# First attention group of a fused two-block kernel: queries and keys computed together behind zeros, x operands ahead of weight splits, second group's attention steps two slots later

## The reference

```python
def fox_mixer(h, w_in, b_f, q_gain, k_gain, w_out):        # h = rms_norm(x, mix_norm)
    q, k, v, f_logit = jnp.split(h @ w_in, [hd, 2 * hd, 3 * hd], axis=-1)
    q = rms_norm(q.reshape(bsz, seq, N_HEADS, HEAD_DIM), q_gain)     # 16 heads of 128
    k = rms_norm(k.reshape(bsz, seq, N_HEADS, HEAD_DIM), k_gain)
    log_f = jax.nn.log_sigmoid(f_logit + b_f)
    cum = jnp.cumsum(log_f, axis=1).transpose(0, 2, 1)
    ...
    s = jnp.einsum('bqhd,bshd->bhqs', qb, k) * scale + (cq[..., :, None] - cum[:, :, None, :])
    return _causal_softmax(s, start, v)                    # then @ w_out
```

## Time and profile before

| | us |
|---|---|
| median of 3 runs (2439.43 to 2442.14) | 2441.04 |
| the profiled execution, its own time | 2437.49 |
| its span, first to last instruction | 2435.7 |
| TensorE matmuls busy | 2411.1 (99%) |
| DVE busy | 1641.1 (67%) |
| ACT busy | 1290.5 (53%) |
| GpSimd busy | 216.9 (9%) |

### The profile page before, as it was taken

The page is one execution under the profiler, slowest core; times in us unless marked ns, Lnnn a source line. Parts: engine busy times, 40 slices in busy tenths (PEclk is TensorE's granted clock), DMA queues, the critical chain, the costliest instruction groups (busy, mean ns, idle before and its releaser), DMA issues. The chain is left out here.

```text
span 2435.7 us, 32611 instructions
## 1 busy us (share of the span) xinstructions
PE 2411.1 (99%) x11468; PEld 2112.1 (87%) x11468; DVE 1641.1 (67%) x1831; ACT 1290.5 (53%) x1723; POOL 216.9 (9%) x365
## 2 busy tenths in 40 slices
PE   8999999999999999999999999999999999999997
PEld 7888888888888888888889888888888888888886
DVE  5666665877777777776877655466566766676666
ACT  6555555655555555554444555555554444444444
POOL 0111101100000000000010100000110000000000
PEclk9999999999999999999999999999999999999999
DMA  7877777888877788767566766568877777777775
GB/s 238 271 215 226 220 220 233 251 238 236 236 237 236 235 233 239 220 191 232 178 203 184 246 192 206 176 225 253 248 234 222 232 225 231 224 229 228 223 233 164
DMA packets 270391, 545.79 MB, mean 224 GB/s; under 512 B 22011, under 2 KB 23395, under 8 KB 270179
## 3 DMA queue, kind: packets, MB, share of 16 engines
q1 hardware_dynamic: 244064, 469.82, 63.6%
q0 software_dynamic: 22192, 70.28, 10.4%
q10 hardware_dynamic: 4051, 4.59, 0.6%
HBM read 508.93 MB, written 35.68 MB: 224 GB/s over the span
## 5 line engine op out<-in xcount | busy, mean ns | idle before, releaser
L1418 DVE TENSOR_TENSOR w_lo<-raw,w_hi 128x1024 fp32r<-128x1024 f32 x887 | 1078.2, 1221 | 666.0 <-ACT w_hi L899 660.6
L899 ACT ACTIVATE w_hi<-raw 128x1024 fp32r<-128x1024 f32 x887 | 934.2, 1056 | 916.4 <-PE acc L498 771.5
L496 PE MATMUL acc<-w_hi,A_hi 128*128 128x512 f32 x1932 | 741.9, 384 | 1.5 <-DVE A_lo L1901 1.0
L497 PE MATMUL acc<-w_lo,A_hi 128*128 128x512 f32 x1932 | 732.2, 379 | 0.0
L498 PE MATMUL acc<-w_hi,A_lo 128*128 128x512 f32 x1932 | 732.2, 379 | 0.0
L496 PEld LDWEIGHTS acc<-w_hi,A_hi 128*128 128x128 f32 x1932 | 365.3, 189 | 53.1 <-DVE A_lo L1901 1.4
L498 PEld LDWEIGHTS acc<-w_hi,A_lo 128*128 128x128 f32 x1932 | 365.1, 189 | 51.8
L497 PEld LDWEIGHTS acc<-w_lo,A_hi 128*128 128x128 f32 x1932 | 365.3, 189 | 50.5
L496 PE MATMUL acc<-w_hi,B_hi 128*128 128x512 f32 x800 | 304.6, 381 | 0.6 <-DVE B_lo L1685 0.6
L496 PE MATMUL acc<-w_hi,C_hi 128*128 128x512 f32 x800 | 303.4, 379 | 0.2 <-DVE w_lo L1418 0.2
L497 PE MATMUL acc<-w_lo,B_hi 128*128 128x512 f32 x800 | 303.2, 379 | 0.0
(11 more groups left out here) (207 smaller groups left out, 1310.0 us busy)
## 6 DMA issues: line engine op xcount, KB each, us to landing
raw<-in_up SPq DMA_DIRECT2D x304, 512.0 KB, 4.5
raw<-in_w SPq DMA_DIRECT2D x271, 512.0 KB, 4.4
raw<-in_down SPq DMA_DIRECT2D x216, 512.0 KB, 4.9
raw<-in_wo SPq DMA_DIRECT2D x64, 512.0 KB, 5.1
turn_rows<-scratch POOLq DMA_DIRECT2D x23, 512.0 KB, 3.2
scratch<-turn_rows POOLq DMA_DIRECT2D x92, 128.0 KB, 5.9
up_rows<-scratch POOLq DMA_DIRECT2D x21, 512.0 KB, 5.3
scratch<-up_rows POOLq DMA_DIRECT2D x84, 128.0 KB, 5.2
```

Of the source, the lines that this page charges most:

```text
L496: pe.matmul(o, hi[:, kt, ts], wh, start=first and kk == 0, stop=False)
L497: pe.matmul(o, hi[:, kt, ts], wl, start=False, stop=False)
L899: act.activation(w_hi[:, q % RING, :], raw[:, q % RING, :], ACT.Copy).then_inc(w_hi_ready, 1)
L1418: dve.tensor_tensor(w_lo[:, q % RING, :], raw[:, q % RING, :], f32(w_hi[:, q % RING, :]), ALU.subtract).then_inc(w_lo_ready, 1)
```

## The change

- Group 0 takes its first 16 slots in turn: query slot s, key slot s (`z1_order`), so each x chunk serves four slots in place of two. Loads follow that order, and x chunks 1, 2, 3 are loaded after slots 2, 5, 8 in place of beside slots 1, 2, 3.
- GpSimd clears `junk` first, and TensorE runs three matmuls on it before anything else.
- x chunk operands on ACT and DVE stand ahead of the split at slots 2, 6, 10; the split of slot 1 stands ahead of x operands 2 and 3; the turn of x tiles 2 and 3 moves from inside slot 0 to ahead of slot 1.
- The forget gate's matmuls move to slot 14, their transposes to 16, the cumulation to 20, the DMA of its result to 21, `spread_gates(0)` to 23. Two small tiles move to another buffer.
- Group 0's query squares move from slot 11 to 16 and norm from 13 to 18; key squares from 16 to 19, norm from 18 to 21.
- In group 1 all attention steps come two slots later, its query squares and norm one slot later, the first gate mask two slots later.

```diff
+        def z1_order(p, first):
+            return (p % 2, p // 2) if first and p < 2 * SPC else divmod(p, SPC)
-        def fox_steps(p, last=False):
-            begun = (2, 4, 6, 8) if last else (3, 5, 7, 9)
+        def fox_steps(p, last=False, late=0):
+            begun = (2, 4, 6, 8) if last else (3 + late, 5 + late, 7 + late, 9 + late)
...
             def fox_body(R, g, first=False):
...
+                for p in range(3 * SPC):
+                    k, s = z1_order(p, first)
+                    if first and p == 0:
+                        first_loads()
+                        continue
+                    load(R, p, a["w1"], s * SLOT_K * P, g * CW + k * D, wait=not (first and p < RING))
+                    if first and p in (2, 5, 8):
+                        load_x((p + 1) // 3)
...
-                    if kk == 0:
-                        pe.wait_ge(x_in[0], 16)
-                        turn_pair(2, turned)
                 m.then_inc(slot_done, 1)
+            pe.wait_ge(zeros_made, 1)
+            for k in range(3):
+                pe.matmul(acc[:, 2, 0:T], junk[:, 0:P], junk[:, 0:T], start=True, stop=True)
             pe.wait_ge(ident_in, 16)
...
                 if p == 1:
+                    pe.wait_ge(x_in[0], 16)
+                    turn_pair(2, turned)
+                if p == 2:
                     pe.wait_ge(turn_dve, TN_X + 1)
...
+                if p in (4, 8, 12):
+                    pe.wait_ge(turn_dve, TN_X + 1 + p // 4)
+                if p in (2, 6, 10):
+                    m = (2, 6, 10).index(p) + 1
+                    pe.wait_ge(x_in[m], 16)
+                    turn(chunk_of_resid(m), TN_X + m)
+                if p == 5:
                     turn_tabs()
-                if p == 9:
+                if p == 14:
                     pe.wait_ge(f_lo, 1)
...
-                if p == 11:
+                if p == 2 * SPC:
                     pe.wait_ge(f_kept, 1)
...
-                if p == 2 * SPC:
+                if p == 20:
                     cumulate()
...
+            act.wait_ge(w_early, 16)
+            act.activation(w_hi[:, 0, 0:CW], raw[:, 0, 0:CW], ACT.Copy).then_inc(w0_hi, 1)
             act.wait_ge(mix_turned, 1)
             chain.link(act.activation(gain[:, G_MIX:G_MIX + KT], acc[:, 3, 0:KT], ACT.Copy))
...
+            split(0, 1 - AHEAD)
             act.wait_ge(turned, 1)
             early_operand(2).then_inc(early_hi, 1)
             early_operand(3).then_inc(turn_act, 1)
-            split(0, 1 - AHEAD)
             split(0, 2 - AHEAD)
-            operand(TN_X + 1, A_hi, JT, G_MIX)
...
-                if p == 2 * SPC + 1:
+                if p == 21:
                     act.wait_ge(cum_kept, 1)
...
-                if p == 2 * SPC + 3:
+                if p == 23:
                     act.wait_ge(cum_out, 32)
                     spread_gates(0)
...
+                    if first and p in (2, 6, 10):
+                        m = (2, 6, 10).index(p) + 1
+                        operand(TN_X + m, A_hi, m * JT, G_MIX)
                     split(R, p)
...
-                        for kind, j in fox_steps(p):
+                        for kind, j in fox_steps(p, late=2 if isinstance(g, int) and g == 1 else 0):
                             fox_step(kind, g - 1, j)
...
-                    if p == SPC + 3:
+                    if p == (2 * SPC if first else SPC + 4 if g == 1 else SPC + 3):
                         head_squares(stage_q, 3 * g + 1)
-                    if p == SPC + 5:
+                    if p == (2 * SPC + 2 if first else SPC + 6 if g == 1 else SPC + 5):
                         head_norm(stage_q, 2 * g + 1)
...
-                    if p == 2 * SPC:
+                    if p == (2 * SPC + 3 if first else 2 * SPC):
                         head_squares(stage_k, 3 * g + 2)
-                    if p == 2 * SPC + 2:
+                    if p == (2 * SPC + 5 if first else 2 * SPC + 2):
                         head_norm(stage_k, 2 * g + 2)
...
+            pool.memset(junk[:, :], 0.0).then_inc(zeros_made, 1)
             pool.memset(nothalf, -0.5).then_inc(filled, 1)
```

More of the change, by code:

```diff
@@ L401, in load, with load_x @@
                 sp.dma_start(raw[:, ring, :].rearrange("p (k n) -> p k n", k=SLOT_K), src).then_inc(landed[ring], 16)
+            def load_x(m):
+                c = slice(m * CW, (m + 1) * CW)
+                sp.dma_start(resid[:, :, c], x[:, :, c]).then_inc(x_in[m], 16)
             def fox_body(R, g, first=False):
-                for k in range(3):
-                    for s in range(SPC):
-                        p = k * SPC + s
-                        if first and p == 0:
-                            first_loads()
-                            continue
-                        if first and p < NCH:
-                            load(R, p, a["w1"], s * SLOT_K * P, g * CW + k * D, wait=False)
-                            c = slice(p * CW, (p + 1) * CW)
-                            sp.dma_start(resid[:, :, c], x[:, :, c]).then_inc(x_in[p], 16)
-                            continue
-                        load(R, p, a["w1"], s * SLOT_K * P, g * CW + k * D)
+                for p in range(3 * SPC):
[6 more added lines that the diff above has]
+                        load_x((p + 1) // 3)
             def first_loads():
@@ L982, in early_operand @@
                                       scale=gain[:, G_MIX + j:G_MIX + j + 1])
-            def early_split(kk):
-                v = slice(kk * CW, (kk + 1) * CW)
-                return act.activation(w_hi[:, 0, v], raw[:, 0, v], ACT.Copy)
-            act.wait_ge(w_early, 16)
-            early_split(0).then_inc(w0_hi, 1)
             act.wait_ge(early_turned, 1)
@@ L1010, in first_steps @@
             def first_steps(p):
-                if p in (0, 1):
-                    operand(TN_X + 2 + p, A_hi, (2 + p) * JT, G_MIX)
                 if p == 2:
-                    act.wait_ge(filled, 3)
-                if 2 <= p <= 5:
-                    square(0, p - 2)
+                    act.wait_ge(zeros_made, 1)
+                if p in (3, 4, 8, 11):
+                    square(0, (3, 4, 8, 11).index(p))
                 if p == 2:
@@ L1083, in fox_pass @@
                             spread_gates(1 + p // 2)
-                        for kind, j in fox_steps(p):
+                        for kind, j in fox_steps(p, late=2 if isinstance(g, int) and g == 1 else 0):
                             fox_step(kind, g - 1, j)
-                    c, s = divmod(p, SPC)
+                    c, s = z1_order(p, first)
                     if s == SPC - 1:
@@ L1507, in _ @@
             early_split(1).then_inc(w_lo_ready, 1)
+            split(0, 1 - AHEAD)
             early_operand(2)
             early_operand(3).then_inc(turn_dve, 1)
-            split(0, 1 - AHEAD)
             split(0, 2 - AHEAD)
-            operand(TN_X + 1, A_hi, A_lo, JT, G_MIX)
             def first_steps(p):
-                if p in (0, 1):
-                    operand(TN_X + 2 + p, A_hi, A_lo, (2 + p) * JT, G_MIX)
-                if p == 5:
+                if p == 11:
                     sum_squares(0)
-                if p == 6:
+                if p == 7:
                     dve.wait_ge(f_hi, 1)
@@ L1549, in first_steps @@
                     m.then_inc(f_z, 1)
-                if p == 13:
+                if p == 18:
                     dve.wait_ge(f_log, 1)
@@ L1596, in fox_pass @@
                 for p in range(3 * SPC):
+                    if first and p in (2, 6, 10):
+                        m = (2, 6, 10).index(p) + 1
+                        operand(TN_X + m, A_hi, A_lo, m * JT, G_MIX)
                     split(R, p)
@@ L1600, in fox_pass @@
                     else:
-                        if p == 0 and g == 1:
+                        if p == 2 and g == 1:
                             dve.wait_ge(levels_made, 1)
```

38 lines of the change are left out of this document (15 added, 23 removed).

## The result

The changed kernel takes 2445.2 us (median of 17 runs, 2442.4 to 2449.8) where the kernel before takes 2441.04 beside it: a ratio of 1.0019, 95% interval 1.0013 to 1.0026. One of the 17 executions of before took 3652.7 us and is left out of the ratio; the others took 2437.9 to 2444.2. Run again on another chip the changed kernel took 2443.6 against 2440.77, ratio 1.0013 (1.0004 to 1.0022). So it is slower, by 4.2 and 2.8 us in the medians of the two sets. That is clear of noise and under the 0.2% (4.9 us) that the prediction took as its measure, though the first interval reaches beyond it.

What follows compares the result with a forecast made beforehand. TensorE, busy 99% of the span, bounds the kernel. Start -3.1 and wait at the scores +5.1 give +2.0 on the profiled 2437.49, 2439.5; with 3.55 from profile to median, 2443.0 us, range 2438.0 to 2446.5.

Steps and rivals of the forecast that it cites:

- rival (2): Query's send through DRAM takes 5.9 us, delaying key's root, split of slot 25 and scores: +4.2, 2445.2 us; chance 0.18.
- The start: TensorE's slots 0 to 4: slot 1 near 11.0 us, slot 4 near 20.0 instead of 25.25, a gain of 3.1 us.
- a slow slot 0: At the start: slot 0 at 1.2 GHz ends near 11.3 us, delaying slot 1 by 0.7 and slot 4 by 0.2.
- Zeros costed at nothing: Three zero matmuls before slot 0: 3.6 us inside TensorE's 5.2 us wait for its first operand, so no cost.
- rival (3): Zeros leave slot 0 at 1.2 GHz and slot 4's load lands no earlier than 16.6: +3.1, 2444.1 us; chance 0.08.
- the byte stream: Order of loads at the start: slot 4's weights land at 15.6 us; slot 4 starting after 21 would prove this wrong.
- The chain of query and key: Group 0's trip through DRAM: query's send near 69 us, bring about 3.7 later, key's root 77.6, its send 80.4.
- The wait: TensorE at the first scores, slot 29: ready at 97.1 us, reached at 92.0, so 5.1 us, about 1 earlier at slot 24.
- Two terms: Cumulated gates before slot 24: DVE copies them near 74.0 us, ACT sends 0.5 later, and they land 5.0 after that.
- The sign that I gave: In the profile: TensorE waits 3 to 5 us at the scores, with ACT idle there for the transfer from qk_rows.
- The 16.1 us from transpose to copy: Key's trip from its transpose to ACT's first copy: 16.1 us with gate rows in flight, 13.1 without.
- DVE's squeeze: Second group, slots 38 to 42: the two-slot shift squeezes DVE by one slot; costed at nothing, at most 0.5 us.

Runs made afterwards that it cites:

- e1: Changed kernel with ACT waiting for the cumulated gates and sending gate row 0 behind the value evacuation, at slot 24; ratio 1.0024 to the kernel before.
- e11: e9 with four zero matmuls in place of three; ratio 1.0017 to the kernel before.
- e3: Changed kernel with the second group's attention steps at their old slots, not two later; ratio 1.0040 to the kernel before.
- e4: Changed kernel with the cumulated gates copied by DVE at slot 19 and sent by ACT at slot 20; ratio 1.0033 to the kernel before.
- e5: Changed kernel with gate rows 1 to 3 loaded at slots 6, 9, 12 of the second group, not 0, 2, 4; ratio 1.0011 to the kernel before.
- e8: Changed kernel run again unchanged, on another chip; 2443.6 us against 2440.77, ratio 1.0013.
- e2: Changed kernel without the three zero matmuls; ratio 1.0042 to the kernel before.
- e6: Changed kernel with the edits of e1, e4 and e5 together and the first gate mask two slots later; ratio 1.0015 to the kernel before.
- e9: Changed kernel with e4's early send, gate rows at slots 27, 32, 36, 40, masks later, second group's shift four slots; ratio 1.0018 to the kernel before.
- e7: e6 with the second group shifted four slots and GpSimd computing the key's root before bringing the query back; ratio 1.0002 to the kernel before.
- e12: Kernel before with the forget gate's steps at their new slots, first mask two slots later, two small tiles moved; ratio 1.0027 to the kernel before.

## Why the prediction was right, and where it was not

The time fell in the range and within 0.2% of before, 2.2 us above the forecast. That is part luck. By the prediction's own division 2445.2 lies in the band of rival (2), the one with a chance of 0.18, and even equals its sum, though its mechanism, a slow send of the query, did not occur; what put the time there are terms that no rival had. By its steps:

**The start: right in mechanism, 1.3 us too good.** The load of slot 4 was the bound I named, and it kept: DVE's low half of chunk 1 was ready at 20.2, where the sum had 19.9. But slot 4 began at 21.31. The step that failed is that a slow slot 0 would cost slot 1 0.7 us and slot 4 0.2. Slot 0 began at 7.00 and needs 12 x 0.43 = 5.2 us at 1.2 GHz, so it ended at 12.2 and not at 11.3, and then 7.8 us of matmuls and the turn were longer than the load. With the higher clock (e1, e11) slots 1 and 4 came at 11.18 and 20.08, 10.92 and 19.89, and slot 24 3.0 and 3.2 us early: the 3.1 of the sum. Zeros costed at nothing: right, they ended at 4.3 and the next thing TensorE waited for was a DMA. What they give differs from run to run; rival (3), which takes this for one of its two conditions, put the start at 2.0 us, and 1.8 were measured. The prediction also gave as a sign that if slot 4 starts later than 21, the byte stream is wrong. It did start later, and the byte stream was right.

**The chain of query and key: right.** The query's send was forecast near 69 and measured at 71.16; 1.3 us of that are the later start, the rest I can't place; bring 3.7 us later, measured 3.66; key's root and send 77.6 and 80.4, measured 79.0 and 81.84; the key's send landed after 3.7 us, its bring began after 4.2. Rival (2), a slow send of the query, did not occur: 3.7 us again in e1, e3, e4, e5, e8 and e11, and 4.4 to 4.5 in e2, e6 and e9, just beyond the 4 us from which it was to decide, but not its 5.9. DVE's split of slot 25 was not what TensorE waited for.

**The wait: right in size, wrong in place.** I had 5.1 us at the scores, 1 us of it earlier at slot 24. TensorE stood 3.5 us at slot 24, was slow for another 1.7, and the scores came without a wait, at 98.65 when the copies had ended at 98.57. Two terms were mis-sized. DVE copied the cumulated gates at 75.39, 1.4 us after the 74.0 of the sum, in step with the start. And their DMA took 6.6 us instead of 5.0, with the weights and the query's bring in flight. That put the end of ACT's wait at 82.8, where the sum had 79.5. The reading that the two waits are one debt, paid wherever it falls due first, is what e1 and e4 show: take the first away, and 4.5 and 7.2 us appear at the second. The sign that I gave, ACT idle at the scores for the transfer from qk_rows, did not show either. The 16.1 us from transpose to copy came out to the tenth, but the key itself took 15.0 of them, and the last 1.2 are ACT's wait for a late tile of weights. The forecast had no such term. So two waits end there close together, and which ends last changes: weights in the changed kernel, e1, e9 and e11, the key in e2, e3, e4, e6, e7 and e8.

**What the sum left out: the clock behind a stall.** A stall of 3.54 us cost 1.7 more. The same followed 2.81 us (1.6, e8), 3.0 (1.8, e3), 3.29 (1.8, e5) and 2.36 us (1.8, e2), each from the ledger between slots 24 and 26. In all fourteen traces, from 20 us to near their end, the clock fell behind every stall of 2.28 us or more and behind none of 1.99 or less, 1.85 us in the kernel before among them. In between it went either way: it fell behind 2.04 (e9), 2.17, 2.20 and 2.21 us and not behind 2.11, 2.16 (e5) and 2.23 us (e12). The forecast reckoned a wait as its length; here a wait of 3.5 us is one of 5.2.

The Trainium skill, "TensorE: Matmul & The Clock Gate", Part 1, says that the lower clock is the default and that activity releases it, and warns that the count of slow matmuls at the start varies from run to run of one kernel. The traces agree: the clock rose near 10.7 us in the kernel before, at about 12.2 in the changed kernel, at 10.4 in e8, which is the same kernel, and ahead of slot 0 in e1. I had used that rule for slot 0's start alone and not asked what it says of the stall I forecast.

**The second group.** I costed DVE's squeeze at 0 to 0.5 us. TensorE waited 1.2 us for probabilities in the changed kernel and 0.6 in e8, and with a shift of 4 slots 2.2 in e7 and 5.1 in e9, where the masks had moved too. That step was too low.

Put together against the profile: -1.8 at the start, +3.5 stall, +1.7 clock, +1.2 probabilities make +4.6, and the ledger has 5.3 at slot 56. Of the remaining 0.7 half is the second wait on L918; the rest I can't place. Between slot 88 and the end another 0.6 us is added; one difference there is a wait for an A_lo near the end, 1.7 us where before has 1.0. The forecast was -3.1 + 5.1 = +2.0.

What stays open: which part of e2's loss is due to the zeros and which to the chance of the order (it is one profile, though its time is the median of five runs); and whether the zeros do anything on average. Slot 24, stalls left out, was 0.9 us early without them and 1.0 to 3.0 early in the nine traces with three (the changed kernel, e8, e1 and e3 to e7, e9). Nor does the moment when the clock rose speak for them: without zeros 10.7, 12.4 and 13.0 us (before, e12, e2), with three ahead of slot 0 in one trace of ten (e1), for a part of slot 0 in another (e5), and from 10.4 to 13.6 in the other eight. No version tried beats the kernel before.

## What to carry to other kernels

Time won ahead of a chain that runs through DMAs is kept only if every step of that chain moves with it: ask of each in-order engine what stands behind the wait for the last transfer, and expect that when one wait is removed the next takes its place. Look at the loads of weights on that engine too: a transfer that isn't on the chain can hold it through them. In this kernel a stall of TensorE of 2.3 to 4.5 us cost its length and about 1.7 us more, and one of 2.0 to 2.25 us sometimes did too. Where of two transfers of like size one is on the critical path, it is worth trying to issue that one first; here its first leg then took 4.2 to 4.9 us instead of 6.3 to 8.9, though no run tested the order alone.

## What the runs showed of the hardware that I had not expected

- Behind a TensorE stall of 2.4 to 3.5 us the granted clock fell to 1.2 GHz (0.59 in the 4 us behind the changed kernel's), 1.6 to 1.8 us lost each time. Stalls of 2.0 to 2.25 us had this behind them in four of seven cases.
- When the clock rises at the start is not fixed by the program: in the same slot 0, behind the same three matmuls of zeros, it was up from the first matmul (e1) or only at the end (the changed kernel), and in two executions of one kernel it rose at 12.2 and at 10.4 us (the changed kernel, e8).
- A send of 512 KB took 3.7 us with a 768 KB load issued 1 us behind it, and 7.1 us with that load issued 0.13 us ahead of it. A gate row took 6.4 us with no other near (e5); two issued 0.6 us apart took 7.8 and 12.2 (changed kernel), and a tile of weights beside them 11.9, against the 5.9 and 9.6 of the earlier trace rows. But a single row beside the key's return took 9.0 too (e9).
- A small DMA of the cumulated gates, 16 partitions to DRAM, took 6.6 us where it took 5.0 before and 4.1 when issued some 4 us sooner (e4), and this, not its size, set when TensorE went on.
